# A decoder-trunk kernel whose input projection becomes three products of rounded halves

## The chip, the cores and the metric

The kernel runs on one core of one Trainium2 chip. The metric is the time of one execution on the device, in microseconds (us); lower is better. The inputs are those of the reference; all data are float32 in memory.

## What is computed

One inference step of one layer: an input projection, a recurrent block (convolution and gated linear recurrence), sparse attention with three branches (compressed, selected pages, sliding window) for 512 prompt tokens and 8 samples, an output projection, and an expert layer (PEER) that takes most of the time. Cut to what matters here:

```python
def layer_forward(x, c, lw, rel_bias, past):
    sh1, sc1, gt1, sh2, sc2, gt2 = ada_mod(c, ada_w, ada_b)        # silu(c) @ ada_w, 1024 -> 6144
    h = rmsnorm(x, norm1_g) * (1.0 + sc1) + sh1
    xr, yg, q, kv_c, kv_s, kv_w, gl = split_columns(h @ w_in)      # the input projection
    ...
    o_c, o_s, o_w, new_win = nsa_sample(q, kv_c, kv_s, kv_w, cache_cmp, cache_sel, cache_win,
                                        page_table, layer, cmp_w, rel_bias)
    xc, new_conv = causal_conv(xr, conv_buf, conv_w, conv_b)
    hs, new_h = rg_lru(xc, h0, lru_wa, lru_ba, lru_wi, lru_bi, lru_lambda)
    o_lru = hs * jax.nn.gelu(yg)
    mixed = jnp.concatenate([rmsnorm(o_lru, ...), rmsnorm(o_att, ...)], axis=-1) @ w_out
    x = x + gt1 * mixed
    h2 = rmsnorm(x, norm2_g) * (1.0 + sc2) + sh2
    ff = peer_ffn(h2, peer_wq, peer_bq, peer_subkeys, peer_u, peer_v)
    x = x + gt2 * ff
```

Each of the 8 samples has 8 pages of 128 rows in the cache of the selected branch, found by `page_table`; a page holds keys (128 floats a row in the kernel's layout) and values (128 floats).

## The kernel before

**Layout.** Activations are kept transposed, 128 features on the partitions and 520 tokens (512 of the prompt, 8 samples) along the free dimension, so that a matrix product goes over 8 blocks k of 128 features and, because a bank of PSUM holds 512 floats, over two halves of 260 tokens. One large SBUF tensor, `arena`, is cut by hand into buffers whose lives do not overlap.

**The engines are five hand-written instruction streams** that wait for each other's semaphores: `sp` (SyncE, issues most transfers), `pool` (GpSimd, issues transfers too), `pe` (TensorE), `act` (ScalarE) and `dve` (VectorE). Nothing is reordered: what stands first on an engine is done first.

**The z stage**, the subject of this case, is a loop of 18 steps n on every engine; step n gives 128 columns of h @ w_in (`zT[:, n, :]`).

- `pe` (line 713): step n takes the weights `win_w` (two slots), multiplies in float32 (line 723; 16 products, which the profile records as 32 instructions), and raises `z_ready`. After it stand two `ada_step`s (line 598), which go on with the conditioning matrix `ada_w` (32 tail pieces, two per step, in two slots), and two `turn_m9`s (line 609), which transpose the rows of two earlier pieces. `turn_m9` waits for `mt_done`, that is, for `shift_m` of DVE two pieces before. At n = 7, 9, 11, 13 two small products for the recurrent gates (`lru_gate`, line 570) stand among them. Step n+1 after such an n waits for `ri_ready`, a Sigmoid of ACT that empties the bank.
- `act` moves the odd z out of PSUM, copies the ada rows (`copy_m9`), and works on the gates; all under one helper, line 1143.
- `dve` moves the even z out (line 1533), adds the bias to the turned ada pieces (`shift_m`, line 1434), and does convolution and recurrence (lines 1456 to 1525). `lru_dve` counts finished recurrences; the fourth is at n = 14.
- `sp` issues, for each n: `w_in[n]` once step n-2 is done, up to three pages of the selected branch (`page_rows`, line 299, keys and values together, 128 x 256 floats), and two tail pieces of `ada_w`, each as its slot comes free. After the loop: the weights of the compression (`load_w1`), the store of `o_kv`, the gates through memory (`gscratch`, `gate_rows`), the window's values (`vwin`).
- `pool` issues pages 32 to 52 during the steps, and pages 53 to 63 when `lru_dve` has reached 4. Each page needs its number from the page table (`value_load`) before its transfer is issued.

**After the z stage** `pe` turns values, forms scores with the cached keys (`strips`, lines 766 and 768; the selected pages' keys with a wait for `pages_sync` and `pages_pool`), with the window's keys, and the compression of the prompt (line 754). Then come the values: `outputs` (line 831), first those of the window after a wait for `win_loaded`, then, behind the prompt's compressed scores (line 854), those of the compressed and selected branches. The latter raises `sel_free`, upon which POOL loads the bias table (`biasT<-rrows`, line 519), for which the prompt's attention waits. After that stage the output projection, the query projection (line 973) and the expert layer follow.

**The query projection already uses products of rounded halves**: ACT copies a float32 tensor to fp32r (`wqh`), which rounds it, DVE subtracts to get the rest (`wql`, line 1779), and PE forms high x high, high x low and low x high with fp32r operands (line 973), of the same shapes as in the z stage.

## Time and profile before

| | us |
|---|---|
| median of 3 runs (1780.49 to 1781.4) | 1780.54 |
| the profiled execution: its time | 1785.46 |
| the profiled execution: its span, first to last instruction | 1783.5 |
| PE busy | 1710.9 (96%) |
| DVE busy | 1272.1 (71%) |
| ACT busy | 648.1 (36%) |
| POOL busy | 375.0 (21%) |

The span is cut in 40 slices of 44.6 us; the z stage, from 73.6 to 246.1 us, lies in slices 2 to 6. The profile gives, for each stretch, the busy time of the engines, the clock that TensorE was granted (1.00 is 2.4 GHz, 0.50 is 1.2 GHz), and the load on the DMA engines. Its chain of waits is followed back from the last instruction: at each step to what released it. A matmul's end is modelled, so neighbouring records overlap; the time of a step is read from the chain, where pieces do not overlap.

### The profile page before, as it was taken

How to read it: one execution, taken by the hardware profiler on the slowest of the kernel's cores; microseconds unless marked ns; L12 is line 12 of the kernel's file. 1: busy time of each engine (PE TensorE's matmuls, PEld its weight loads, DVE VectorE, ACT ScalarE, POOL GpSimd, SP SyncE). 2: the span in 40 equal slices, each digit the busy share in tenths (PEclk: the TensorE clock that was granted, in tenths of full speed). 3: DMA queues.
4: the chain of work that ended last, by engine and by line, in shares of the span. 5: the costliest groups of instructions: out<-in, count | busy, mean ns of one | idle time of the engine just before them, and what ended most of it. 6: DMA issues, size and time to landing. Idle time of an engine off the chain costs nothing.

```text
span 1783.5 us, 30052 instructions
## 1 busy us (share of the span) xinstructions
PE 1710.9 (96%) x11385; PEld 1579.7 (89%) x11385; DVE 1272.1 (71%) x2648; ACT 648.1 (36%) x1023; POOL 375.0 (21%) x372
## 2 busy tenths in 40 slices
PE   7999998778899999999899999999999999999997
PEld 5688777447799999999899999999999999999997
DVE  0213335573386789999899999976888787878786
ACT  1113321672142233334344444433333333333332
POOL 3201010000000001111354444441232222222220
PEclk9999996799899999999999999999999999999999
DMA  9776661600242227776699999999999999999991
GB/s 343 248 233 234 216 214 62 237 1 1 99 179 87 90 88 257 236 232 221 226 353 380 378 372 388 385 383 400 404 398 331 356 337 355 335 356 339 342 324 72
DMA packets 178950, 467.84 MB, mean 262 GB/s; under 512 B 20515, under 2 KB 92707, under 8 KB 177294
## 3 DMA queue, kind: packets, MB, share of 16 engines
q1 hardware_dynamic: 130974, 290.20, 45.9%
q0 software_dynamic: 45120, 173.61, 26.5%
q10 hardware_dynamic: 2736, 2.49, 0.5%
q8 instruction: 68, 1.11, 0.2%
q14 instruction: 52, 0.43, 0.1%
HBM read 408.86 MB, written 64.17 MB: 265 GB/s over the span
## 4 chain that ended last, share of the span: by engine, by line
PE 76%; DVE 12%; DMA 9%; ACT 2%; issue 1%; ACTq 1%; SPq 0%; POOL 0%; DVEq 0%
PE ps L1100 29%; PE ps L986 18%; PE ps L723 7%; PE ps L973 5%; DMA xT<-in_u,gidx 4%; PE ps L926 3%; DVE xT L1823 2%; DVE ul L1775 2%; PE ps L625 2%; ACT arena L1143 1%; PE ps L598 1%; PE ps L1079 1%; DVE oh L1925 1%; PE ps L902 1%; DVE oh L1918 1%
## 5 line engine op out<-in xcount | busy, mean ns | idle before, releaser
L1775 DVE TENSOR_TENSOR ul<-raw,uh 128x1024 fp32r<-128x1024 f32 x256 | 311.8, 1223 | 110.3 <-ACT uh L1143 108.8
L986 PE MATMUL ps<-hh,uh 128*128 128x392 f32 x1024 | 357.1, 349 | 1.7 <-DVE ul L1775 1.7
L986 PE MATMUL ps<-hl,uh 128*128 128x392 f32 x1024 | 349.6, 341 | 0.0
L986 PE MATMUL ps<-hh,ul 128*128 128x392 f32 x1024 | 347.6, 339 | 0.0
L1100 PE MATMUL ps<-ah,ul 128*128 128x392 f32 x1000 | 341.6, 342 | 0.0
L1100 PE MATMUL ps<-al,uh 128*128 128x392 f32 x1000 | 340.8, 341 | 0.0
L1100 PE MATMUL ps<-ah,uh 128*128 128x392 f32 x1000 | 339.6, 340 | 1.3 <-DVE al L1994 1.2
L1143 ACT ACTIVATE uh<-raw 128x1024 fp32r<-128x1024 f32 x256 | 269.8, 1055 | 105.1 <-PE ps L1100 88.5
L530 POOL DMA_INDIRECT xT<-in_u,gidx x128 | 176.7, 1380 | 548.6 <-DVE zg L1823 333.2
L530 POOL DMA_INDIRECT xT<-in_v,gidx x128 | 138.0, 1078 | 377.4 <-DVE vacc L2008 355.4
L986 PEld LDWEIGHTS ps<-hh,uh 128*128 128x128 f32 x1024 | 192.3, 188 | 3.7 <-DVE ul L1775 2.0
L1143 ACT ACTIVATE zbuf<-ps 128x392 f32<-128x392 f32 x128 | 63.9, 499 | 359.5 <-PE ps L986 359.4
L986 PEld LDWEIGHTS ps<-hl,uh 128*128 128x128 f32 x1024 | 192.7, 188 | 0.0
L986 PEld LDWEIGHTS ps<-hh,ul 128*128 128x128 f32 x1024 | 192.5, 188 | 0.0
L1100 PEld LDWEIGHTS ps<-ah,uh 128*128 128x128 f32 x1000 | 187.8, 188 | 2.0 <-issue 1.5
L1100 PEld LDWEIGHTS ps<-al,uh 128*128 128x128 f32 x1000 | 187.7, 188 | 0.0
L1100 PEld LDWEIGHTS ps<-ah,ul 128*128 128x128 f32 x1000 | 187.7, 188 | 0.0
L1823 DVE CUSTOM_DVE_ANT_0 xT<-xT,hg 128x1024 f32<-128x1024 f32 x128 | 156.1, 1220 | 23.0 <-DMA xT<-in_u,gidx 22.7
L2008 DVE SCALAR_TENSOR_TENSOR vacc<-xT,ag,vacc 128x1024 f32<-128x1024 f32 x127 | 162.5, 1280 | 0.6
L1143 ACT ACTIVATE ah<-zin 128x392 fp32r<-128x392 f32 x128 | 68.2, 533 | 239.6 <-DVE zin L1990 237.8
L723 PE MATMUL ps<-arena 128*128 128x260 f32 x576 | 136.1, 396 | 3.5 <-DVE arena L1429 2.0
L723 PEld LDWEIGHTS ps<-arena 128*128 128x128 f32 x576 | 111.7, 197 | 21.7 <-DMA arena<-in_w_in 3.6
(359 smaller groups left out, 2080.8 us busy)
## 6 DMA issues: line engine op xcount, KB each, us to landing
raw<-in_uT SPq DMA_DIRECT2D x128, 512.0 KB, 5.7
raw<-in_v SPq DMA_DIRECT2D x128, 512.0 KB, 6.5
zs<-zbuf SPq DMA_DIRECT2D x128, 196.0 KB, 6.0
gw<-stage POOLq DMA_DIRECT2D x28, 896.0 KB, 11.2
gr<-gw SPq DMA_DIRECT2D x32, 784.0 KB, 8.3
zin<-zs SPq DMA_DIRECT2D x128, 196.0 KB, 6.0
arena<-in_ada_w SPq DMA_DIRECT2D x32, 512.0 KB, 4.4
arena<-in_w_in SPq DMA_DIRECT2D x18, 512.0 KB, 6.7
```

Source lines behind the costliest of these rows:

```text
L530: pool.indirect_dma_start(out=gb[:, s, :], out_offset=None, in_=table, in_offset=bass.IndirectOffsetOnAxis(ap=gidx[:, n:n + 1], axis=0)).t ...
L598: last = mm(ps[32 * j:32 * j + 32, bank, 0:width], cT[:, 2 * j + kk, :], rhs(2 * j + kk), start=(kk == 0), stop=(kk == 1))
L625: last = mm(ps[g * HD:(g + 1) * HD, 2 + 2 * c + h, 1 - m:257 - m], w1p[:, c * 16 + m * 8 + j, :], xv[:, h, :, c, g, j, :], start=(m == 0 a ...
L723: last = mm(ps[:, 2 * (n % 2) + h, 0:HALF], win_w[:, (n % 2) * KD + k, :], hT[:, k, h * HALF:(h + 1) * HALF], start=(k == 0), stop=(k == K ...
L926: last = mm(ps[:, 2 + 2 * (c % 3) + h, 0:HALF], wout[:, k, c * P:(c + 1) * P], zT[:, k, h * HALF:(h + 1) * HALF], start=(k == 0), stop=(k ...
L973: last = mm(ps[:, b + h, 0:HALF], weights[w](k), moving[m](k)[:, h * HALF:(h + 1) * HALF], start=(first and n == 0 and w == 0 and m == 0), ...
L986: last = mm(ps[:, bank, 0:DN], w[x][:, k * P:(k + 1) * P], m[:, k, G0:TOK], start=(k == 0 and x == 0 and m is hh), stop=(k == KD - 1 and x ...
L1100: last = mm(ps[:, dc, 0:DN], w[:, q, cols], m[:, q, :], start=(first and w is uh and m is ah), stop=False)
L1143: return act.activation(out, in_, f, **kw)
L1775: tt(ul[:, i % 4, :], raw[:, i % 4, :], uh[:, i % 4, :].bitcast(F32), SUB).then_inc(S["lo_done"], 1)
L1823: dve.tensor_tensor_reduce(gb[:, n % 4, :], gb[:, n % 4, :], hg[:, :], 1.0, 0.0, MUL, ADD, zg[:, n:n + 1]).then_inc(S["ttr_done"], 1)
L2008: stt(vacc[:, :], gb[:, n % 4, :], ag[:, n:n + 1], vacc[:, :], MUL, ADD).then_inc(S["acc_step"], 1)
```

## The change

Steps 1 to 17 of the z stage use fp32r halves; step 0 remains float32. `h_hi` and `wh` are made by ACT (`high_w`), `h_lo` and the low weights by DVE (`low_w`, in place of the loaded weights); the weights have three slots, and SP loads `w_in[n+1]` where it loaded `w_in[n]`. To make room, the keys and values of the pages have buffers of their own, and only the keys (128 x 128 floats) are loaded in the z stage: 32 pages by SP, 11 by POOL during the steps, and 21 by POOL after the fourth recurrence. The values come behind the stage, 32 pages by SP after `vwin` and 32 by POOL after its keys. The store of `o_kv` moves behind SP's value pages. The window's outputs on PE now wait for all value pages. Window keys and window values change places in memory, and some semaphores are shared.

```diff
+        win_w = [at(o, KD, P) for o in (13520, 14544, 32080)]
+        selk, selv = at(17680, NB * PAGES, P), at(25872, NB * PAGES, P)
@@ sp @@
-            for n in range(2):
-                load(win_w[:, n * KD:(n + 1) * KD, :], io["w_in"][n], w_l[n])
+            sp.wait_ge(S["hid_ready"], 2)
+            for n in range(3):
+                load(win_w[n], io["w_in"][n], w_l[n])
...
             for n in range(2, ZC):
                 sp.wait_ge(S["z_ready"], n - 1)
-                load(win_w[:, (n % 2) * KD:(n % 2 + 1) * KD, :], io["w_in"][n], w_l[n % 2])
-                sp.wait_ge(S["hid_ready"], 2)
+                if n + 1 < ZC:
+                    load(win_w[(n + 1) % 3], io["w_in"][n + 1], w_l[(n + 1) % 3])
                 for m in range(3 * (n - 2), min(3 * (n - 1), 32)):
-                    page_rows(sp, sel[:, m, :], io["pool_s"], m, S["pages_sync"])
+                    page_rows(sp, selk[:, m, :], io["pool_s"], m, S["pages_sync"], slice(0, P))
...
             load_w1(sp, 0, S["w1k_loaded"])
-            sp.wait_ge(S["z_moved"], ZC)
-            load(io["o_kv"], zT[:, KC:ZC, :], S["kv_stored"])
-
             sp.wait_ge(S["gates_ready"], 2)
...
             load(vwin, io["win_v"].rearrange("b (c p) f -> p (b c) f", p=P), S["win_loaded"])
+            for m in range(32):
+                page_rows(sp, selv[:, m, :], io["pool_s"], m, S["win_loaded"], slice(P, 256))
+            sp.wait_ge(S["z_moved"], ZC)
+            load(io["o_kv"], zT[:, KC:ZC, :], S["kv_stored"])
@@ pool @@
-            for n in range(32, 53):
-                pool.wait_ge(S["z_ready"], 5 + (n - 32) // 3)
-                page_rows(pool, sel[:, n, :], io["pool_s"], n, S["pages_pool"])
+            for n in range(32, 43):
+                pool.wait_ge(S["z_ready"], 5 + (n - 32) // 2)
+                page_rows(pool, selk[:, n, :], io["pool_s"], n, S["pages_pool"], slice(0, P))
             pool.wait_ge(S["z_ready"], 13)
             load_w1(pool, 1, S["w1v_loaded"])
             pool.wait_ge(S["lru_dve"], 4)
-            for n in range(53, 64):
-                page_rows(pool, sel[:, n, :], io["pool_s"], n, S["pages_pool"])
+            for n in range(43, 64):
+                page_rows(pool, selk[:, n, :], io["pool_s"], n, S["pages_pool"], slice(0, P))
+            pool.wait_ge(S["z_ready"], ZC)
+            for n in range(32, 64):
+                page_rows(pool, selv[:, n, :], io["pool_s"], n, S["pool_loaded"], slice(P, 256))
@@ pe @@
+            def products(b, weights, moving, ks, ready=None, base=0, every=1):
+                for n, k in enumerate(ks):
+                    if ready is not None and k % every == 0:
+                        pe.wait_ge(ready, base + k // every + 1)
+                    for w, m in ((0, 0), (0, 1), (1, 0)):
+                        for h in range(2):
+                            last = mm(ps[:, b + h, 0:HALF], weights[w](k), moving[m](k)[:, h * HALF:(h + 1) * HALF],
+                                      start=(n == 0 and w == 0 and m == 0), stop=(n == len(ks) - 1 and w == 1))
+                return last
...
+                    pe.wait_ge(S["wql_done"], n)
+                    last = products(2 * (n % 2), [lambda k: win_hi[n % 2][:, k, :], lambda k: win_lo[n % 3][:, k, :]],
+                                    [lambda k: h_hi[:, k, :], lambda k: h_lo[:, k, :]], range(KD),
+                                    ready=S["hl_ready"] if n == 1 else None)
...
-            pe.wait_ge(S["win_loaded"], 16)
+            pe.wait_ge(S["win_loaded"], 16 * 33)
+            pe.wait_ge(S["pool_loaded"], 48 + 16 * 32)
@@ act @@
+            def high_w(n):
+                act.wait_ge(w_l[n % 3], 16 * (n // 3 + 1))
+                if n >= 3:
+                    act.wait_ge(S["z_ready"], n - 1)
+                fn(win_hi[n % 2], win_w[n % 3], ACT.Copy).then_inc(S["rounded"], 1)
+            for k in range(KD):
+                act.wait_ge(S["h_ready"], k + 1)
+                fn(h_hi[:, k, :], hT[:, k, :], ACT.Copy).then_inc(S["hh_ready"], 1)
+                if k == 1:
+                    high_w(1)
+            high_w(2)
...
             for n in range(1, ZC):
+                if n + 2 < ZC:
+                    high_w(n + 2)
@@ dve @@
+            def low_w(n):
+                dve.wait_ge(S["rounded"], n)
+                tt(win_lo[n % 3], win_w[n % 3], win_hi[n % 2].bitcast(F32), SUB).then_inc(S["wql_done"], 1)
+            for k in range(KD):
+                dve.wait_ge(S["hh_ready"], k + 1)
+                tt(h_lo[:, k, :], hT[:, k, :], h_hi[:, k, :].bitcast(F32), SUB).then_inc(S["hl_ready"], 1)
+                if k == 1:
+                    low_w(1)
...
             for n in range(0, ZC, 2):
...
                    0.125 if QC <= n < QC + 4 else 1.0, None, MUL).then_inc(S["z_moved"], 1)
+                if n + 2 < ZC:
+                    low_w(n + 2)
+                if n == 2:
+                    low_w(n + 3)
...
                 if 8 <= n <= 14:
                     recur((n - 8) // 2)
+                if n != 2 and n + 3 < ZC:
+                    low_w(n + 3)
```

The order on two engines. First DVE at step 6: the move of z out of PSUM (L1533 before, L1576 now), `shift_m` (L1434, now L1468), then the convolution. Before:

```order
L1533 TENSOR_SCALAR arena<-ps 128x520 [waits dve_step,z_moved,z_ready]
L1434 TENSOR_TENSOR mT<-ps,par 128x9 [waits mt_ready] x4
L1456 TENSOR_SCALAR arena<-arena,par 128x520
L1459 SCALAR_TENSOR_TENSOR arena<-arena,par 128x511 [waits dve_step]
L1460 SCALAR_TENSOR_TENSOR arena<-arena,par 128x8
```

and now:

```order
L1576 TENSOR_SCALAR arena<-ps 128x520 [waits z_moved,z_ready]
L1487 TENSOR_TENSOR wl<-arena,wh 128x1024 [waits rounded]
L1468 TENSOR_TENSOR mT<-ps,par 128x9 [waits mt_ready] x4
L1499 TENSOR_SCALAR arena<-arena,par 128x520
L1502 SCALAR_TENSOR_TENSOR arena<-arena,par 128x511 [waits dve_step]
L1503 SCALAR_TENSOR_TENSOR arena<-arena,par 128x8
```

The subtraction of the low weights (L1487), which waits for ACT's rounding, has come between the move and `shift_m`.

Second, SP behind the loop of steps (`in_cmp_w` is `load_w1`, `in_win_v` is `vwin`). Before:

```order
L295 DMA arena<-in_cmp_w 64x2048
L305 DMA out_o_kv<-arena 128x3120 [waits z_moved]
L305 DMA gscratch<-gates 8x24 [waits gates_ready]
L305 DMA gate_rows<-gscratch 16x3 [waits att_in,gate_stored]
L305 DMA gate_rows<-gscratch 16x3 x3
L305 DMA arena<-in_win_v 128x32x128 [waits z_ready]
L305 DMA out_o_h<-arena 128x36 [waits lru_dve]
```

and now:

```order
L304 DMA arena<-in_cmp_w 64x2048
L314 DMA gscratch<-gates 8x24 [waits gates_ready]
L314 DMA gate_rows<-gscratch 16x3 [waits att_in,gate_stored]
L314 DMA gate_rows<-gscratch 16x3 x3
L314 DMA xT<-in_win_v 128x32x128 [waits z_ready]
L307 TENSOR_LOAD cst
L307 ISA x2
L308 ISA
L308 DMA arena<-in_pool_s 128x128
```

The store of `o_kv` has gone from here to behind 32 such groups of four rows, each of which reads a page number and issues the values of one page.

## Rows read from the trace of the kernel before

**Rows 1.** The page: shares of the chain that ended last, by engine.
```profile
PE 76%; DVE 12%; DMA 9%; ACT 2%; issue 1%; ACTq 1%; SPq 0%; POOL 0%; DVEq 0%
```

**Rows 2.** The chain, 60 to 345 us: start, us, what (x instructions).
```profile
100.85 7.21 PE ps L723 x32
...
149.38 7.11 PE ps L723 x32
...
194.68 1.05 PE ps L598 x32
...
210.93 9.10 PE ps L723 x32
220.03 0.02 issue
...
246.14 1.01 PE ps L598 x32
...
250.36 1.85 PE ps L766 x16
...
283.18 4.89 PE ps L831 x80
...
302.58 0.28 issue
302.87 8.93 DMA arena<-rrows
```

**Rows 3.** The chain in the query projection, two steps of products of rounded halves.
```profile
503.66 5.97 PE ps L973 x48
...
515.36 5.77 PE ps L973 x48
```

**Rows 4.** PE in order of time, step 6: start, us, instructions [idle before <-releaser].
```profile
128.44 8.97 PE L723 MATMUL ps<-arena 128*128 128x260 f32 x32 [1.48 <-DMA arena<-in_w_in]
```

**Rows 5.** Windows: A:B, us, busy PE, PEld, DVE, ACT, POOL, clock, DMA share, GB/s.
```profile
130.00:132.00 2.00, 2.00 (x7) 1.50 (x6) 0.00 (x0) 0.00 (x0) 0.00 (x0) 0.50 1.01 391
```

**Rows 6.** DVE in order of time, behind step 8, which ended at 156.50.
```profile
156.53 0.70 DVE L1533 TENSOR_SCALAR arena<-ps 128x520 f32<-128x520 f32 x1 [14.14 <-PE ps L723]
157.15 0.23 DVE L1434 TENSOR_TENSOR mT<-ps,par 128x9 f32<-128x9 f32 x2
```

**Rows 7.** ACT, copies of weights to fp32r, 486 to 500 us: min/median/max ns, first to last.
```profile
L1143 ACT ACTIVATE wqh<-arena x2: 1039/1049/1059, 489.7 to 496.2; 128x1024 fp32r<-128x1024 f32 x2
```

**Rows 8.** DVE in order of time, query projection: the low halves of weights.
```profile
498.22 1.22 DVE L1779 TENSOR_TENSOR wql<-arena,wqh 128x1024 fp32r<-128x1024 f32 x1
```

**Rows 9.** ACT in order of time, behind step 7, which ended at 146.07.
```profile
146.11 0.60 ACT L1143 ACTIVATE arena<-ps 128x520 f32<-128x520 f32 x1 [6.78 <-PE ps L723]
...
148.03 0.69 ACT L1143 ACTIVATE arena<-ps,par 128x520 f32<-128x520 f32 x1
```

**Rows 10.** Line 305, window 168.0 to 168.4 us: the landing of one `w_in`.
```profile
DMA to landing us min/median/max: 8.2/8.2/8.2
```

**Rows 11.** Line 305, window 196.6 to 197.3 us: the landing of one `w_in`.
```profile
DMA to landing us min/median/max: 12.5/12.9/13.3
```

**Rows 12.** Waits of SP's queue: engine, line, waited for: us, times, longest.
```profile
SPq L305 <- DMA gscratch<-gates: 8.8, 1, 8.8
```

**Rows 13.** SP in order of time, behind the z stage.
```profile
258.28 1.71 SPq L305 DMA_DIRECT2D gate_rows<-gscratch  x4
...
261.03 5.70 SPq L305 DMA_DIRECT2D out_o_h<-arena  x1
```

**Rows 14.** SP in order of time, early in the kernel: eight pages in a row.
```profile
18.99 8.04 SPq L299 DMA_DIRECT2D arena<-in_pool_c  x8
```

**Rows 15.** POOL in order of time: the first and the last of 11 pages.
```profile
227.82 0.58 POOL L299 DMA_DIRECT2D arena<-in_pool_s  x1 [31.78 <-issue]
...
239.68 0.54 POOL L299 DMA_DIRECT2D arena<-in_pool_s  x1 [0.63 <-issue]
```

**Rows 16.** Line 299, window 226 to 245 us: the landing of these pages.
```profile
DMA to landing us min/median/max: 2.2/3.3/5.6
```

## What the change was predicted to do

> **What bounds the kernel now.** I read the page first, then the chain of waits in order of time, then each engine's own order in the z stage. By the page PE carries 76% of the chain [rows 1], so a shorter product is worth its time wherever nothing else comes late. In the z stage the chain is PE almost without a gap: step after step of 7.11 to 7.21 us [rows 2], with the conditioning products between. Two steps are slower: step 6 (8.97 us, behind 1.48 us of waiting for weights [rows 4]) and step 14 (9.10 us [rows 2]). In both the granted clock had fallen to 0.50, the lower of the two levels, right after PE had waited [rows 5]. Step 17 ends at 246.14, which I call Z; the cached scores start at 250.36 (Z + 4.2), the value products at 283.18 (Z + 37.0), and 19.4 us later, at 302.58, `sel_free` lets POOL load the bias table, which ends the chain of this part [rows 2]. So the z stage is bound by PE, and behind it `sel_free` hands on whatever is late, unchanged, to the rest: nothing after it has slack, since 8.93 us of a lone transfer follow at once [rows 2].
>
> **The change, part by part**, against the profiled span of 1783.5 us. (The profiled execution took 1785.46 us, 4.9 more than the median of the runs; I add the difference that I find to the median.)
>
> a) *Products.* 48 fp32r instructions of the same shape take 5.97 us in the query projection where other products stand before them, as here, and 5.77 behind the expert products [rows 3]. 17 steps x (7.14 - 5.97) = -19.9 us; with 5.77 it would be -23.3. The first row is the nearer. The Trainium skill (TensorE: Matmul & The Clock Gate, "Back-to-back issue gap") gives N/2.4 + 2.5 ns between matmuls, 111 ns for 260 columns, so by estimate 5.3 us a step; the rows show 5.97/48 = 124 ns. By that rule the step would save 0.65 us more, 11 us in all; the rows decide.
>
> b) *Weights a step earlier.* The wait before step 6 and its slow clock go: -(1.48 + 8.97 - 7.11) = -3.3 us [rows 2, 4].
>
> c) *A new wait at even steps.* After step n ends, DVE moves z out and then does `shift_m` at once, 0.65 us after the end; PE needs that for `turn_m9` 1.01 us after it [rows 2, 6], so today it is hidden with 0.2 us to spare. Now `low_w(n+2)` stands between, and it waits for ACT's `high_w(n+2)`, which itself may start only when step n is done. The chain is 0.05 + 1.05 [rows 7] + 0.05 + 1.22 [rows 8] + 0.23 [rows 6] = 2.6 us, so PE waits 2.6 - 1.05 = 1.55 us at n = 4, 6, 8, 10, 12 and 14: +9.3 us. Behind that DVE's queue (shift, convolution, recurrence) moves by as much, which it can bear.
>
> d) *The clock.* The only wait of this length in a step, 1.48 us, was followed by clock 0.50 and cost 1.86 us more [rows 4, 5]. Six such waits: between 0 and 11.2 us. Step 14 is the other slow step, behind a longer wait for `ada_w`. I take half, +5.6.
>
> e) *Gates.* At n = 7, 9, 11, 13 ACT rounds weights (1.05 us) before the move and the Sigmoid (behind the load of its table) that frees the bank for step n+1. That Sigmoid ends at 148.72, step 8 starts at 149.38 [rows 2, 9]: 0.66 us of slack, so 1.05 + 0.02 - 0.66 = 0.41 us each, +1.6. The other `high_w` (odd n of 1 to 5, 15) hide: nobody waits for z, which has two banks.
>
> f) *Late weights.* `high_w(n+2)` needs its weights at the end of step n, a step earlier than PE did. They are issued about 1.5 to 3 us into the step's period of 7.6 to 9.7 us and land within 8.2 us where window keys go with them [rows 10]: some 1.3 us late for step 12's weights, 0.3 for step 6's. +1.6.
>
> g) *Step 13.* `w_in[15]` is issued about 2 us after step 12, together with POOL's compression weights, and lands 12.9 us later [rows 11]. ACT waits for it before it moves z 13: 2.0 + 12.9 + 1.05 + (148.03 + 0.69 - 146.11) = 18.5 us from the end of step 12 to step 14; today 210.93 - 194.68 = 16.25 [rows 2, 7, 9]. Less what a, c and e count there (0.8): +1.5.
>
> Up to Z: -19.9 - 3.3 + 9.3 + 5.6 + 1.6 + 1.6 + 1.5 = -3.6 us (-9.2 if the clock holds).
>
> h) *Pages behind the stage.* POOL takes (239.68 - 227.82)/10 = 1.19 us a page, most of it the reading of its number, not the bytes [rows 15]. All but one of the ten intervals are 1.155; I use that. It starts 7.8 us after step 14 (227.82 - 220.03), now 1.7 later by c, and has 21 keys instead of 11: the last is issued 9.5 + 20 x 1.155 + 0.5 = 33.1 us after step 14 and lands 3.3 later [rows 16], Z + 12.3 (step 14 to Z is now about 24.1). PE asks for it at Z + 4.2, so it waits 8.1 us; its own work from there (32.8 us, some 2 more at the low clock) then reaches the value products at Z + 47. POOL's 32 value pages are issued without a pause behind: 9.5 + 52 x 1.155 + 0.5 + 3.3 - 24.1 = Z + 49.3. SP: load of weights and `gscratch` issued by Z + 2.6; its landing took 8.8 us with the `o_kv` store ahead [rows 12], I take 5 without it; `gate_rows` and `vwin` 2.75 (258.28 to 261.03); then the issue behind `vwin` took 5.70 us where it is by itself well under 1 (the queue was full) [rows 13], and I expect the first page to meet the same; 32 pages of (8.04 - 0.34)/7 = 1.10 us [rows 14]; landing 3.3. Sum: 2.6 + 5 + 2.75 + 5.7 + 35.2 + 3.3 = Z + 54.5. SP's is last, so the value products start at Z + 54.5 instead of Z + 37.0: +17.5. The 19.4 us behind stay. Bounds: +10 if only PE's own key wait counts, +12.3 if POOL's pages are last, +21 if `gscratch` takes its 8.8 still. `o_kv`, `o_h` and `o_conv` go behind the pages; they must land before the prompt's attention 10 us behind `sel_free` and have over 15 us.
>
> Initial halves (8 copies, 8 subtractions, two roundings) lie beside step 0 (to 82.6 us) and the gate products: no cost; uncovered it would be a microsecond.
>
> **Sum:** -3.6 + 17.5 = +13.9: 1780.5 + 13.7 = 1794.
>
> **The rivals.**
> 1. *Faster: the pages are not waited for.* Pages of half the size might be issued faster. It decides when POOL needs under 0.92 us a page (values by Z + 37) and SP under 0.56. Then only the z stage counts: -3.6 to -9.2, 1771 to 1777. For it: half the bytes. Against: 0.62 us of POOL's 1.155 is idle between issues [rows 15], which bytes don't touch. Chance 0.07.
> 2. *No change: the even steps don't wait.* If ACT and DVE round early enough, c and d go: -18.5 + 17.5 = -1.0, 1779.5. Against: `high_w` waits for the step's own end, so it can't be early. With the clock holding and POOL's pages last: 13.9 - 5.6 - 5 = +3, 1783.8. Together 0.16.
> 3. *Slower still: the clock falls at every even step* (+5.6) and `gscratch` is as slow as today (+3.8): 1803. Chance 0.12.
> 4. *The products are no faster than float32*: +20, 1814. Rows 3 speak against; 0.01.
>
> **How the numbers follow.** Forecast 0.64, the rest as said. The likeliest case is the sum, 1794. The range goes from 1781 (clock holds, SP's queue not full, 5.77 us a step) to 1806 (rival 3 and late landings). A measurement can tell 0.2%, 3.6 us, from no change: faster (under 1777) 0.07, within 0.15, slower 0.78.
>
> **What would show it.** Steps 1 to 17 of 5.8 to 6.0 us at clock 1.00; PE waiting for `mT` of DVE 1.5 us at even steps from 4 to 14, and a slow step behind some of them; waits of 0.4 us for ACT before steps 8 to 14; a wait of 7 to 9 us for POOL's pages before line 766's wide products; one of 3 to 8 us for SP's pages before the value products, which start 50 to 57 us behind the stage; the same 19.4 us and the same kernel from there. I am wrong if PE finds the pages there, if `shift_m` is not waited for, or if the later stages differ.

## The result

The changed kernel takes 1799.03 us (median of 4 runs, 1795.27 to 1804.85), the kernel before 1780.97 us beside it (4 runs, 1780.49 to 1784.76). The ratio is 1.0116 with a 95% interval of 1.0089 to 1.0143: 18 us slower, where 14 were forecast, and inside the range. The profiled execution of the changed kernel is the fastest of its four: 1795.27 us, span 1793.6 us, that is 10.1 us over the span of 1783.5 before, which was a long execution (4.9 us over its median).

The page's shares of the chain, to hold against [rows 1]:

```profile
PE 79%; DVE 8%; DMA 6%; SPq 2%; issue 2%; ACT 2%; ACTq 1%; POOL 0%; DVEq 0%
```

SPq, the queue of SyncE, is new at 2%. The chain from 60 to 345 us shows where (start, us, what), against [rows 2]. Line 735 is the product of halves, 48 instructions a step; 613, 585 and 624 are the conditioning products, the LRU gate and `turn_m9`; 861 the value outputs.

```profile
84.88 5.96 PE ps L735 x48
...
115.34 7.38 PE ps L735 x48
...
150.93 1.07 ACT wh L1162
152.02 1.23 DVE wl L1487
153.24 0.16 DVE mT L1468 x2
...
153.47 0.58 PE ps L624 x4
154.05 7.40 PE ps L735 x48
...
193.51 11.49 DMA arena<-in_w_in
...
206.63 1.14 PE ps L585 x4
...
208.68 7.50 PE ps L735 x48
...
240.08 1.05 PE ps L613 x32
...
242.34 6.74 DMA gscratch<-gates
...
251.03 0.80 SPq L314
...
253.08 4.46 SPq L308
...
294.35 4.96 PE ps L861 x80
...
313.93 8.89 DMA arena<-rrows
```

A step is 5.96 us where it is undisturbed, against 7.11 to 7.21 before. Six steps (5, 7, 9, 11, 13 and 14) take 7.3 to 7.5; step 13 is off the chain, which passes it by the landing of `w_in[15]`. The piece at 150.93 is the detour of an even step: step 8 has ended, ACT rounds weights, DVE subtracts, only then comes the `mT` that PE wants. Z, the end of step 17, is at 240.08 instead of 246.14; from there the chain runs through SP: the gates' store to DRAM, `vwin`, one issue of 4.46 us, and page after page until the value outputs start at 294.35 (Z + 54.3). `sel_free` comes 19.3 us later (19.4 before), and the rest, from the load of the bias table on, takes 1479.7 us as against 1480.6 before.

The waits of PE from 60 to 316 us (line waited for: us, times, longest):

```profile
PE ps L624 <- DVE mT L1468: 10.9, 7, 2.2
PE ps L861 <- DMA arena<-in_pool_s: 9.5, 1, 9.5
PE ps L797 <- DMA arena<-in_pool_s: 6.8, 1, 6.8
...
PE ps L585 <- ACT arena L1162: 2.0, 1, 2.0
```

None of the first three stood in the trace before. And the windows (busy PE, PEld, DVE, ACT, POOL, then the granted clock, DMA share, GB/s) inside step 5, whose `turn_m9` had waited 1.63 us at 114.75, and at the key strips behind their wait of 6.8 us:

```profile
116.00:118.00 2.00, 2.00 (x14) 2.00 (x12) 1.93 (x4) 0.00 (x0) 0.00 (x0) 0.61 1.13 322
118.00:120.00 2.00, 2.00 (x11) 2.00 (x11) 1.12 (x4) 0.00 (x0) 0.00 (x0) 0.54 1.16 186
120.00:122.00 2.00, 2.00 (x19) 2.00 (x18) 0.00 (x0) 0.00 (x0) 0.00 (x0) 1.00 0.83 243
...
249.00:258.00 9.00, 6.88 (x32) 1.28 (x36) 0.00 (x0) 0.00 (x0) 4.25 (x8) 0.50 0.70 190
```

PE is busy throughout, but does 11 to 14 matmuls in 2 us instead of 19: the slow steps are slow by the clock, which lies near its lower level (0.50) for some 3 us. A wait is not always followed by this: behind step 14 PE waited 1.63 us too, and step 15 took 5.86 us.

### The profile page after: what moved, and what is told of

Its sections match the earlier page's. It is cut to its first block, busy times and chain, and to the rows that moved or that the text cites. A ratio compares the mean times of both kernels' runs of the same rounds, so it can differ in the third digit from the quotient of the medians.

```text
span 1793.6 us, 31047 instructions
## 1 busy us (share of the span) xinstructions
PE 1693.8 (94%) x11657; PEld 1578.3 (88%) x11657; DVE 1297.7 (72%) x2673; ACT 668.0 (37%) x1048; POOL 392.2 (22%) x404
## 4 chain that ended last, share of the span: by engine, by line
PE 79%; DVE 8%; DMA 6%; SPq 2%; issue 2%; ACT 2%; ACTq 1%; POOL 0%; DVEq 0%
PE ps L1119 27%; PE ps L1005 25%; PE ps L735 10%; PE ps L957 3%; PE ps L1098 2%; DMA raw<-in_v 2%; PE ps L640 2%; DMA arena<-in_w_in 1%; ACT arena L1162 1%; PE ps L933 1%; DVE ul L1824 1%; SPq L308 1%; PE ps L613 1%; DVE arena L1690 1%; SPq L307 1%
## 5 line engine op out<-in xcount | busy, mean ns | idle before, releaser
L545 POOL DMA_INDIRECT xT<-in_v,gidx x128 | 138.3, 1081 | 377.5 <-DVE vacc L2057 356.1
L1162 ACT ACTIVATE arena<-arena,cst 128x128 f32<-128x128 f32 (+4 forms) x139 | 73.7, 565 | 69.3 <-DVE cst L1694 28.9
L2039 DVE TENSOR_TENSOR zin<-zin,gr 128x392 f32<-128x392 f32 x128 | 71.7, 560 | 13.2 <-DMA zin<-zs 13.2
```

Source lines behind the costliest of these rows:

```text
L545: pool.indirect_dma_start(out=gb[:, s, :], out_offset=None, in_=table, in_offset=bass.IndirectOffsetOnAxis(ap=gidx[:, n:n + 1], axis=0)).t ...
L1162: return act.activation(out, in_, f, **kw)
L2039: tt(z, z, gr[:, s % 4, :].rearrange("p (c j t) -> p c j t", j=JB, t=TC)[:, :, jj, :], MUL).then_inc(S["mul_done"], 1)
```

## The experiments

The prediction's theory has two halves: the steps gain 20 us and give most of it back (waits for DVE at even steps, the clock behind them, late weights), and the pages behind the stage cost 17.5 us, SP's queue last. The rivals: the steps lose their gain to something else (landing of weights alone); the pages are slow because of the transfers and not the queue; the wait for keys counts too. All kernels of a batch ran on one chip beside the kernel before; times across batches are compared by their ratio to it. Spans and positions are of one execution each, medians of several.

| kernel | median us (range, runs) | ratio to before [95%] | step 1 starts | Z | outputs start |
|---|---|---|---|---|---|
| before (first profile) | 1781.0 (1780.5 to 1784.8, 4) | 1 | 84.5 | 246.1 | 283.2 |
| changed, again | 1799.3 (1798.0 to 1801.7, 5) | 1.0121 [1.0101, 1.0140] | 83.7 | 242.2 | 297.1 |
| e1 shift first | 1787.5 (1786.2 to 1793.3, 6) | 1.0058 [1.0038, 1.0078] | 84.3 | 233.8 | 289.0 |
| e2 no values | 1782.5 (1773.4 to 1792.1, 12) | 1.0023 [1.0004, 1.0043] | 86.6 | 242.8 | 284.2 |
| e3 fill | 1792.0 (1788.0 to 1796.1, 6) | 1.0083 [1.0061, 1.0104] | 82.8 | 233.9 | 289.0 |
| e4 late w1 | 1795.2 (1793.5 to 1799.5, 6) | 1.0099 [1.0074, 1.0124] | 86.7 | 238.9 | 295.2 |
| e5 early gates | 1792.3 (1789.2 to 1797.3, 6) | 1.0078 [1.0052, 1.0104] | 86.3 | 242.4 | 293.7 |
| e6 split keys | 1799.4 (1793.9 to 1803.9, 6) | 1.0113 [1.0086, 1.0140] | 84.3 | 243.7 | 298.7 |
| e7 pages and order | 1767.0 (1761.2 to 1768.3, 6) | 0.9936 [0.9913, 0.9959] | 83.3 | 221.6 | 262.0 |
| e8 before, late w1 | 1776.7 (1771.9 to 1783.9, 12) | 0.9985 [0.9965, 1.0005] | 83.4 | 236.0 | 275.0 |
| e9 full width | 1776.5 (1773.6 to 1781.4, 12) | 0.9980 [0.9965, 0.9994] | 86.5 | 239.1 | 276.7 |
| e10 w1 later | 1767.6 (1763.2 to 1776.1, 6) | 0.9919 [0.9895, 0.9944] | 86.9 | 224.1 | 271.8 |
| e11 pages only | 1780.4 (1776.2 to 1787.6, 12) | 0.9995 [0.9979, 1.0012] | 87.0 | 250.1 | 286.9 |

### The changed kernel again

> The changed kernel itself, once more on the chip of the runs beside it, to compare with. Expected 1795 to 1801 us, 14 to 20 above the kernel before. Its runs so far spread over 10 us; if the spread comes from TensorE's clock behind the waits of the even steps, a slower profile has a longer product step behind more of steps 4, 6, 8, 10, 12 and 14.

1.0121, as before. In this execution Z comes 158.4 us after step 1's start (155.3 in the first profile). The difference lies behind step 13, in one landing (chain, 190 to 226 us):

```profile
193.02 13.40 DMA arena<-in_w_in
...
208.04 2.10 PE ps L585 x4
```

`w_in[15]` needs 13.40 us here and 11.49 in the first profile; step 14 starts 10.2 us behind the end of step 13 instead of 6.0. That is a part of what the median holds and the first profile doesn't. The guess that a slower execution has more slow steps is not borne out: five are slow here (5, 7, 9, 11 and 14), and step 13 runs at full clock behind a wait of 1.97 us.

### e1: DVE's shifts first

```diff
 zT[:, n, :] = ps ...                       # DVE moves z out, even n
-if n + 2 < ZC:
-    low_w(n + 2)
-if n == 2:
-    low_w(n + 3)
 ...
 for i in range(max(4 * (n // 2) - 8, 0), 4 * (n // 2) - 4):
     shift_m(ADA_HEAD + i)
+if n + 2 < ZC:
+    low_w(n + 2)
+if n == 2:
+    low_w(n + 3)
```

> One edit: DVE does shift_m before low_w(n+2), as before the change. My theory (the turned pieces wait for DVE behind the low weights): PE's six waits for mT (10.9 us in the profile of after) go, and with them the product steps of 7.3 to 7.5 us (five, 1.4 us too long each); the stage ends 14 to 18 us earlier, at 223 to 226 us, everything behind it keeps its distance from the stage's end (value products 54 us behind it), and the time is 1780 to 1785 us. Rival (the loads of weights and ada_w set the pace of the stage): less than 5 us are won, since PE then waits for weights or for ada_w instead.

Of the 10.9 us for `mT` 0.4 are left, steps 5, 7, 9 and 11 are 5.9 to 6.0 us long, and the time falls by 11.8 us (ratio 1.0121 to 1.0058), to 1787.5 where 1780 to 1785 was expected. Step 1's start to Z takes 149.5 us, 5.8 and 8.9 less than in the two profiles of the changed kernel. PE now waits for others:

```profile
PE ps L585 <- ACT arena L1162: 7.8, 3, 5.1
PE ps L613 <- DMA arena<-in_ada_w: 2.4, 1, 2.4
```

Line 585 is the LRU gate, which wants the bank that ACT frees; ACT stands in `high_w` before it, waiting for `w_in` (13.33 us to land in this run). Steps 12 and 14, behind its waits of 2.2 and 5.1 us, take 7.8 and 7.7 us. So the mechanism of terms c and d holds; of the 18.2 us that they measure in the first profile (10.9 of waits, 7.3 of slow steps) 11.8 came back by the medians; the rest went to late weights and the slow steps behind them, as far as one execution tells. The pages keep their distance to Z (55.3 us).

### e3: PE kept busy through the wait

```diff
+if 4 <= n <= 14 and n % 2 == 0:
+    pe.wait_ge(S["z_moved"], n)
+    if n >= 8:
+        pe.wait_ge(S["ri_ready"], n - 6)
+    ... 16 products of h_hi with h_hi into the next step's bank, unused
 if n >= 3:
     for i in (2 * n - 6, 2 * n - 5):
         turn_m9(ADA_HEAD + i)
```

> Adds work: at even steps 4 to 14 PE does 16 fp32r products (128x260, not used, into the banks that the next step will overwrite) between ada_step and turn_m9, where it would wait for DVE. DVE's late shift_m stays. 16 x 0.12 = 1.9 us against waits of 1.5 to 2.2 us. If the slow steps behind come from PE's waiting (clock 0.50 after it), they are back at 5.9 us: -1.45 x 5 = -7, +0.1 to 0.4 for each filler, so 4 to 7 us faster than the changed kernel. If the slow steps had another cause (the transfers at that time), they stay and the kernel is 0 to 3 us slower.

Work was added, the wait for DVE's subtraction stands, and the kernel is 7.3 us faster. The chain, 108 to 160 us (line 779 is the filling):

```profile
111.17 2.11 PE ps L779 x16
...
113.62 5.87 PE ps L735 x48
...
127.91 2.11 PE ps L779 x16
...
130.57 5.86 PE ps L735 x48
```

The steps behind the even ones are short again, so their 1.4 us each came from PE's idleness before them and not from the transfers at that time, the rival named. This settles what term d is. Step 14 stays slow (7.1 us): it stands behind ACT's wait, which was not filled.

### e4: the compression weights later

```diff
-pool.wait_ge(S["z_ready"], 13)
-load_w1(pool, 1, S["w1v_loaded"])
 pool.wait_ge(S["lru_dve"], 4)
 for n in range(43, 64):
+    if n == 48:
+        load_w1(pool, 1, S["w1v_loaded"])
     page_rows(pool, selk[:, n, :], ...)
```

> The changed kernel with one edit on POOL: the second half of cmp_w1 (1 MB) is not loaded at step 13's end (z_ready 13) but behind the first five of the 21 late key pages, some 20 us later. It tests term g, that this load shares the DMA engines with w_in[15] and w_in[16] and makes steps 13 and 14 wait for them. My theory: step 13's wait (11.49 us of w_in in the chain, PE waiting 2.0 us at its first ada product) and the slow step 14 (7.5 us) shrink together by 2 to 5 us, so Z (the end of step 17) comes at 236 to 239 instead of 240 to 242, and the time falls by as much: 1795 to 1797 beside 1799. Rival: the wait at step 13 is the step's own length, since w_in[n + 1] is requested only when step n - 2 is done and takes 7 to 8 us to land and 1.05 us to be rounded; then w_in still lands late, and Z and the time move by under 1.5 us.

The time falls by 4 us (intervals overlap: 1.0099 against 1.0121). The trace is clearer. `w_in[15]` lands 7.90 us after its issue, and behind step 13 nothing waits but 0.45 us:

```profile
186.78 7.90 DMA arena<-in_w_in
...
197.83 5.86 PE ps L735 x48
...
206.99 0.45 issue
207.44 6.01 PE ps L735 x48
```

From step 13's end to step 14's start it takes 3.8 us; 6.0 and 10.2 in the two executions with the early load, 12.1 in e1. From step 1's start to Z it is 152.2 us, 3.1 and 6.2 less than in the two profiles of the changed kernel. The 1 MB of `cmp_w1` beside the 0.5 MB of `w_in[15]` was what made the latter late: with the early load it lands after 11.4 to 13.4 us in five executions (changed kernel twice, e1, e3, e11), without it after 6.4 to 7.9 us in three (e4, e7, e10). Of it term g had counted only 1.5 us. Here too the clock held at places: steps 11 and 13 take 5.9 us behind waits of 1.63 and 2.11 us.

### e8: the same edit on the kernel before

> The kernel before with the one edit on cmp_w1 that took 4 us off the changed kernel: its second half is issued by POOL behind five of the 11 late page loads instead of at step 13's end. It tells whether that load's cost belongs to the change or was there all along. My theory: in the kernel before a step lasts 7.11 us, w_in[n] has one more microsecond to land, and PE waited little for it behind step 13, so at most 1.5 us go: 1777 to 1779 where the kernel before gives 1778.5. Rival: the load costs the kernel before as much as the changed one (3 to 6 us): then 1773 to 1775, and the changed order of the pages would owe part of its gain to something that the kernel before could have too.

3 us by the medians, but the interval reaches past 1 (0.9985 [0.9965, 1.0005]): between theory and rival, and not settled. Its profile is of use for something else. The chain, 60 to 250 us, at steps 6 and 14, to hold against [rows 2, 4]:

```profile
119.09 7.14 DMA arena<-in_w_in
126.28 7.28 PE ps L723 x32
...
202.80 7.13 PE ps L723 x32
```

Step 6 is the same code as before, and here it takes 7.28 us instead of 8.97, behind a wait of 0.36 us instead of 1.48: its weights landed 1.1 us sooner. The slow step 6 is a matter of the single execution. From step 1's start to Z it is 152.6 us here and 161.7 in the first profile of the kernel before, 9.1 us more. Some 3 of them are at step 6 and some 6 between steps 12 and 15, where the edit acts; but the medians differ by 3 us only, so that first profile was a long execution there too (or e8's a short one, 2.4 us under its median).

### e2: no value pages

The value pages are not loaded; PE takes the key pages in their place, so the amount of its work is unchanged.

> Leaves out the loading of all 64 value pages of the selected branch (PE multiplies by the keys of these pages in their place, the same shapes); nothing else. My theory: the value products start when PE arrives by itself, 44.8 us behind the stage's end instead of 54.3, and the time falls by 9 to 10 us, to 1786 to 1790 us; the wait of 6.8 us for POOL's keys stays, and so a difference to the kernel before of 6 to 10 us, half of it in that wait. Rival (the values' traffic slows the rest of the attention too, or the stage's own loss is the greater part): it falls by over 12 us, or by under 6.

The wait before the outputs is gone and the time falls by 16.8 us, more than the 9 to 10 expected and within the rival's range. From Z to `sel_free` it is 58.1 us instead of 74.0. The row of windows, 255 to 260 us, of the changed kernel again and of e2, shows a part of the excess:

```profile
255.00:260.00 5.00, 5.00 (x28) 0.66 (x24) 0.00 (x0) 0.00 (x0) 2.21 (x5) 0.50 0.96 279
```

```profile
255.00:260.00 5.00, 5.00 (x36) 0.84 (x28) 0.00 (x0) 0.00 (x0) 0.00 (x0) 0.71 0.92 246
```

Both wait 6.8 us for the last key pages, then e2 has the clock back sooner, and PE's own work ends at Z + 41.5 instead of Z + 44.7. The outputs take 16.6 us, not 19.0. So some 10 of the 16 us are the wait, and what the other 6 come from is open. It need not be the missing values: e3, which loads them, has PE's own work done at Z + 41.5 too. Nor need it be the idle stretch before the outputs: they take 16.5 us behind 12.5 and 13.7 us of waiting in e1 and e4, and 19.4 without any wait in the kernel before.

### e5 and e6: which queue is it

```diff
 # e5: SP, in the loop instead of behind it
+if n == 6:
+    sp.wait_ge(S["gates_ready"], 2)
+    load(io["gscratch"]..., gates[0:NB, 4, :], S["gate_stored"])
+if n == 16:
+    sp.wait_ge(S["gate_stored"], 16)
+    sp.wait_ge(S["att_in"], 1)
+    for c in range(4): load(gate_rows[32 * c:32 * c + 16, :], ...)
 # e6: SP takes keys 54 to 63 from POOL
+if n == 17:
+    sp.wait_ge(S["lru_dve"], 4)
+    for m in range(54, 59): page_rows(sp, selk[:, m, :], ...)
 load_tail(2 * n - 4); load_tail(2 * n - 3)
+if n == 17:
+    for m in range(59, 64): page_rows(sp, selk[:, m, :], ...)
```

> The changed kernel with one edit on SP: the gates' way through DRAM (gscratch, then gate_rows) goes into the loop (step 6 and step 16) instead of standing behind the stage. SP then comes to vwin and its 32 value pages at about Z + 0.5 instead of Z + 11, and their last lands at Z + 44; POOL's last page lands at Z + 48 as before, so the value outputs start at Z + 48 instead of Z + 54.3. My theory: the time falls by about 6 us, to 1793, and all of it is in the wait before the outputs (9.5 to 10 us becomes about 4). Rival 1: POOL's pages are as slow as they are because of its own pace, but SP's and POOL's pages share the DMA engines, and earlier SP pages only slow POOL's: then the outputs start at Z + 51 or later and under 3.5 us are saved. Rival 2: the outputs wait for something else than pages (DVE's softmax of the gates): no saving.

> The changed kernel with one edit on two queues: ten of POOL's 21 late key pages are issued by SP in step 17's turn of the loop. The wait of the key strips (6.8 us on POOL's pages) goes, and POOL's value pages end 11 us sooner, but SP's value pages, which stand behind the gates' way through DRAM and vwin, end where they did. My theory: the value outputs start at Z + 54 as before, the 6.8 us come back as a longer wait before them (about 16 us instead of 9.5), and the time stays within 2 us of 1799. Rival: SP's late start is not what counts and the page loads as a whole are limited by the DMA engines or by POOL; then the outputs start at Z + 46 to Z + 50 and the time falls by 4 to 8 us.

PE's waits, e5 (230 to 320 us) and then e6 (line 868 there is the value outputs):

```profile
PE ps L799 <- DMA arena<-in_pool_s: 11.0, 1, 11.0
...
PE ps L863 <- DMA arena<-in_pool_s: 5.5, 1, 5.5
```

```profile
PE ps L868 <- DMA arena<-in_pool_s: 21.2, 1, 21.2
```

e6 came out as the theory has it: the key wait is gone, the wait before the outputs grew to 21.2 us, they start at Z + 55.0 and the time stays. The key wait was in the shadow of SP's queue.

e5 moves the outputs to Z + 51.3, not Z + 48, though its time falls by 0.43% (7.7 us, with an uncertainty of about 6; the spans are 2.2 and 5.6 us shorter than the two of the changed kernel). What came between is the first rival, in a form that I had not named. SP's pages (line 308, 243 to 300 us; duration ns min/median/max, first and last start):

```profile
L308 SPq DMA_DIRECT2D arena<-in_pool_s x32: 332/333/10443, 246.7 to 291.9; - x32
```

`vwin` is now issued at 245.08, right behind the 1 MB of `cmp_w1`, and the first page's issue behind it stands for 10.4 us instead of 4.5; POOL's key pages come later too, so the key strips start at Z + 15.2 instead of Z + 11.0. SP's first page is issued 8.7 us sooner behind Z than before (Z + 4.3 instead of Z + 13.0), and the longer issue takes 6.0 of them back. That the transfers met is my reading of these times; no run separates it.

### e7: pages on three queues, and the three edits on the steps

To e1, e4, e5 and e6 together e7 adds:

```diff
 # POOL, with its keys in the loop: values 57 to 63, whose place is free
+if n >= 36: page_rows(pool, selv[:, n + 21, :], ..., n + 21, ...)
 # behind the stage
-SP: vwin, values 0 to 31      POOL: values 32 to 63
+SP: values 0 to 19, vwin      POOL: values 32 to 56
+ACT, behind the cached scores' Exp: values 20 to 31
```

> The changed kernel with the four order edits together (DVE shifts before low_w(n + 2); cmp_w1 late; the gates' way through DRAM in the loop; key pages split) and the value pages spread over three queues: seven (57 to 63, whose place is free before the stage) on POOL during steps 8 to 14, 25 on POOL and 20 on SP behind the stage, 12 on ACT while it waits for the key strips, and vwin behind SP's. All values should have landed by Z + 35, PE's own work before the outputs ends at about Z + 37 without the key wait, so the outputs start at Z + 37 instead of Z + 54: -17 us; the steps give -9 us as in the run with the shift first. Expected: 1773 us, 1768 to 1779, so faster than both kernels. Rival: the step gain doesn't add to the page gain, or key and value pages in flight together slow w_in or the key strips as much: then about 1785.

1767.0 us, one under the range expected, ratio 0.9936 [0.9913, 0.9959]: faster than the changed kernel by 33 us (1.85% by the ratios) and than the kernel before by 12. POOL's seven early values were issued between 127 and 153 us, before step 10 started, not during steps 8 to 14. PE in order of time, behind step 17, which ended at 221.58:

```profile
231.09 2.74 PE L808 MATMUL ps<-arena 128*32 128x512 f32 x16
...
256.53 0.36 PE L856 MATMUL ps<-ident,arena 128*63 128x64 f32 x2 [2.03 <-ACT arena L1173]
...
262.04 0.65 PE L872 MATMUL ps<-arena 8*32 8x128 f32 x8
```

The key strips (line 808) wait for nobody, and no wait is recorded before the value outputs (line 872). They start at Z + 40.5, where the expectation said 37: part of PE's own work ran at the low clock (0.60 and 0.72 from 225 to 235 us), and as it ends `vwin`, now behind SP's 20 pages, has just landed; the chain goes through it:

```profile
251.03 10.96 DMA xT<-in_win_v
```

In e9 and e11, which have the same order, PE waits 2.1 and 1.5 us for it. No step is longer than 6.0 us, and behind ACT's waits of 1.58 and 1.81 us the clock held. ACT issued its 12 pages in 12.28 us; the Exp behind them found its input ready at 243.4 us and started at 246.0, so the pages cost ACT 2.6 us.

The Trainium skill (DMA: Bandwidth & Descriptors, "Issuing engines are not separate DMA queues") says that engines that issue concurrently share the same 16 DMA engines and save only the sequencers' time. The traces agree, and show that the sequencers' time, which the page calls usually small, is not small here: a queue takes 1.0 to 1.2 us for each page of 64 KB, and with the pages on three queues the outputs start 14 us nearer to Z. That holds for the page edits together (e11 has them without the others); no run has the three queues alone.

### e10: the compression weights later still

> The best version with cmp_w1's second half behind all of POOL's late key pages instead of behind the fifth, so that the last two slices of ada_w (9.17 us to land, PE waits 1.5 and 1.7 us for them behind step 17) have the DMA engines more to themselves. My theory: 1 to 3 us off that place, 1764 to 1766; the load is needed by PE only 24 us behind step 17. Rival: the slices are late because SP issues them behind five key pages and they wait for their slots; then nothing changes, or the later cmp_w1 delays the value pages and PE waits for them: 1767 to 1769.

1767.6 us and no difference to e7 that can be measured. The profiled execution is the longest of its six (1776.1). The key pages came later in it (PE waits 4.18 us for them) and the outputs start at Z + 47.7 instead of Z + 40.5, while the waits for `ada_w` behind step 17 are gone: given back within 10 us.

### e11: do the two halves add?

> The changed kernel with the three edits on pages and gates together (gates in the loop, key pages split, value pages over three queues), but with DVE's order and cmp_w1 as the change has them. It tells whether the page gain and the step gain add. My theory: Z stays at 240 to 242, the value outputs start at Z + 41 instead of Z + 54.5, so 13 to 14 us go: 1785 to 1787 beside 1799. Rival: the page edits also move the steps (pages 57 to 63 are now in flight beside w_in during steps 8 to 14, and gate_rows at step 16), in either direction; then Z moves by more than 2 us and the time falls outside 1783 to 1789.

Median 1780.4 (0.9995 [0.9979, 1.0012]), outside the expected 1783 to 1789, 22 us below the changed kernel by the ratios where 13 to 14 were expected. The profiled execution is a long one of its 12 (span 1785.9) and has the outputs at Z + 36.8, but Z only at 250.1. Its weights land late behind step 13, and steps 12 to 15 take 7.4 to 7.8 us (chain):

```profile
199.33 13.21 DMA arena<-in_w_in
...
214.16 2.10 PE ps L596 x4
216.92 7.72 PE ps L746 x48
```

Z comes 163.1 us after step 1's start, 4.7 and 7.8 more than in the two profiles of the changed kernel. Whether the edits on pages do this (the rival) isn't shown: `w_in[15]` took 13.40 us in one of those too, POOL's early values were all issued before step 10, and the median speaks for the other direction. As far as the medians tell, the parts add: by ratios -0.63% for e1, -0.22% for e4 and -1.26% for e11 make -2.1%, and e7 is -1.85%.

### e9: the best version without the three products

```diff
-products(2 * (n % 2), [win_hi..., win_lo...], [h_hi..., h_lo...], ...)
+for k in range(KD):
+    for h in range(2):
+        mm(ps[:, 2 * (n % 2) + h, 0:HALF], win_w[n % 3][:, k, :],
+           h_hi[:, k, h * HALF:(h + 1) * HALF].bitcast(F32), ...)
 # high_w and low_w only count their semaphores on
```

> The best version so far (shift first, cmp_w1 late, gates early, pages over three queues) with the products of steps 1 to 17 put back to one full fp32 product per half (16 instead of 48 instructions a step) and ACT and DVE no longer rounding or subtracting the weights. The input's rounded half stands in for the input, so the low parts of input and weights are left out of the result; the time of the instructions is that of the kernel before. It measures what the three products are worth once nothing else is in their way. My theory: 17 steps x (7.11 - 5.96) = 19.5 us of product time come back, of which up to 6 us are hidden, since w_in lands late at steps 8, 10, 12 and 14 of the best version: 1781 to 1787 beside 1767. Rival: the steps are bound by w_in's landing and by ACT, not by PE's products; then under 8 us come back (1775 or less) and the gain of the best version is one of page order alone.

1776.5 us: the three products are worth 7.8 us by the ratios to the kernel before (0.9980 against 0.9936) and 8.9 us beside e10, which ran with it, so less than the theory's 14 at least and at the rival's bound of 8. The chains, 60 to 250 us, around steps 13 and 14, first e9, then e7 (160 to 200 us):

```profile
195.48 7.11 PE ps L768 x32
205.90 7.16 PE ps L768 x32
```

```profile
181.98 7.53 DMA arena<-in_w_in
...
191.14 1.14 PE ps L596 x4
...
193.19 6.00 PE ps L746 x48
```

At full width a step ends and the next starts 3.3 us later (195.48 + 7.11 = 202.59, to 205.90); with short steps the weights' landing is in the chain and the same gap is 5.8 us. From step 1's start to Z it is 152.7 us at full width and 138.3 with three products: 14.4 us, of the 19.5 that the instructions save. In the part behind, the short version gives another 3 back (outputs at Z + 40.5, at full width Z + 37.5: the pages were started by things that don't move with Z), which leaves 11.4 by the traces. And e9, with every edit on order and pages but full-width products, lies 0.2% under the kernel before: without the short products those edits bring about as much as the split of the pages had cost, and little more.

## Why the prediction was right, and where its terms were off

**Direction and size.** 1794 was forecast, 1799 measured. The two mechanisms are the ones that were named, and each was shown by taking it away: e1 and e3 for the steps, e6, e2 and e5 for SP's queue. That the number came so near is in part luck. The profile that the forecast was read from was long, 161.7 us from step 1's start to Z, and the first profile of the changed kernel was short, 3.8 us under its median. Between these two executions the change cost 10.1 us, 3.8 less than forecast; between the medians it cost 18, 4 more. (The sum of 13.9 went into the time as 13.7; it makes 1794.4.)

- *a, products*: 5.96 us a step, as taken from [rows 3], and 5.86 behind turned pieces; no step came near the estimate of 5.3 us. The Trainium skill (TensorE: Matmul & The Clock Gate, "Back-to-back issue gap") gives its formula for an isolated matmul, not for a stream of matmuls with weight loads. e9 shows what the sum must not do: count all 19.5 us when the weights' landing and ACT are close behind.
- *b, step 6*: -3.3 us was wrong as a gain against the median. The slow step of [rows 4, 5] belonged to that one execution, which was itself 4.9 us over the median of its runs; e8 shows the same step at 7.28. Step 14's 9.10 us went into the same base, 7.13 in e8, whose edit lies near it. The difference of spans was then added to the median. With the undersized g this can account for the 5 us that the forecast lacks; single executions can't show it.
- *c, waits at even steps*: 1.55 us each forecast, 1.63 measured where the weights are in time, so 9.8 for 9.3 us. Right. The 10.9 us of the profile hold 0.9 more for late weights at steps 6 and 12 (term f) and a seventh wait of 0.2.
- *d, clock*: five slow steps on the chain of about 1.45 us more each, 7.3 us; 5.6 forecast, half of the bounds. They stand behind the waits of steps 4, 6, 8 and 10 and behind ACT's at step 13; the slow step behind step 12 is off the chain, and behind step 14's wait of 1.63 us the clock held. e3 gives 7.3 us for it. That half the bound was taken was a guess, and it hit near: in the seven executions with the late shift (changed kernel twice, e2, e4, e5, e6, e11) 32 of the 42 waits at even steps were followed by a slow step. What decides it isn't shown.
- *e, gates*: 0.45 us at steps 8, 10 and 12; 0.41 forecast.
- *f, g, late weights*: 3.1 us forecast. f was 0.3 us at step 6, as forecast, and 0.5 instead of 1.3 at step 12. Behind step 13 alone it was 2.2 us in the first profile (6.0 - 3.8) and 6.4 in the second. The load that collides with `w_in[15]` was named, the lengthening of its landing was taken from [rows 11] and not asked for its spread: 11.49, 13.33 and 13.40 us in three runs.
- *Z*: -3.6 forecast, -6.1 and -3.9 in two profiles.
- *h, pages*: outputs at Z + 54.5 forecast, Z + 54.3 measured. Within it: the gates' landing 6.7 (5), the blocked issue 4.5 (5.7), 1.11 us a page (1.10), keys waited for 6.8 (8.1), PE's own work done at Z + 44.8 (Z + 47). The errors cancel. That the queue is full behind `vwin` was an inference; the traces bear it out. In all 14 profiles the next issue on SP, whatever it moves, stands for 4.3 to 6.3 us (10.4 in e5) and ends when 610 to 700 of `vwin`'s 1024 packets have started (781 in e5).
- *Behind*: 19.3 for 19.4 us, the rest 0.9 us shorter.

**The rivals.** 1 (pages not waited for) fell with the first trace; e2, where only the values are not waited for, came to the time of the kernel before (1.0023). 2 (even steps don't wait) fell too, and e1 puts its price at 11.8 us. 3, slower still, came close: most even steps are followed by a slow one, and the median of 1799 lies between the forecast and its 1803. 4 fell with the first step of 5.96 us.

**Left open.** Why e11 is faster in its median than its trace explains, what 6 of e2's 16.8 us come from, why the clock holds behind about a quarter of the waits, and how much of e8's 3 us is real. As far as it is, the kernel before could have had it too, and e7's lead of 12 us shrinks by as much.

## What to carry to other kernels

When a step gets shorter, list for each engine what stands between the end of the step and the next thing that PE needs, and put the new work behind it: the change lost 11.8 us to two lines in the wrong order on DVE. A transfer split in two costs its queue a second fixed time for each part (1.1 us a page here, 64 of them), and that is only free if the queue has the room; count the issues per queue before the bytes. And a gain taken from a single execution is to be held against the spread of the runs: a slow step in the profile before may be that execution's own.

## What the hardware showed that was not expected

- Waits of PE of 1.6 to 2.5 us in an otherwise dense stream were followed in 32 of 42 cases, 1 to 2 us later, by some 3 us at clock 0.5 to 0.6, which cost 1.4 us and more each; in the other ten, and behind waits of 1.6 to 1.8 us in e7, the clock held. Sixteen useless products of 2.1 us in their place cost less than the idleness (e3, -7.3 us).
- An issue on SP behind `vwin` (2 MB, by its shape 4096 pieces of 512 bytes, in the trace 1024 packets of 2 KB) stood for 4.3 to 6.3 us in 13 profiles, and for 10.4 us when a 1 MB load had been issued just before `vwin` (e5).
- A load of 0.5 MB (`w_in[15]`) took 11.4 to 13.4 us to land beside one of 1 MB from another queue, in five executions, and 6.4 to 7.9 us without it, in three; step 14 started up to 6.4 us later for it (changed kernel again, against e4).
